# Attention in a hybrid layer: turns of the weight tiles in the row halves of the array, value products in bursts of two units

## What is computed

```python
def _stick_breaking(q, k, v):
    q = q.astype(f32) * (d ** -0.5)
    for blk in range(S // Q_BLOCK):
        z = jnp.einsum('bthd,bshd->bhts', qb, kb)
        strict = jnp.arange(t1)[None, :] < jnp.arange(t0, t1)[:, None]
        log_beta = jax.nn.log_sigmoid(z)
        log_keep = jnp.where(strict, jax.nn.log_sigmoid(-z), 0.0)
        after = lax.cumsum(log_keep, axis=3, reverse=True) - log_keep
        A = jnp.where(strict, jnp.exp(log_beta + after), 0.0)
        outs.append(jnp.einsum('bhts,bshd->bthd', A, vb))
```

## Time and profile before

| | |
|---|---|
| median of 3 runs | 3558.57 us (3555.73 to 3559.9) |
| profiled execution, span from first to last instruction | 3554.5 us |
| PE busy in it | 3472.8 us, 98% |
| DVE, ACT, POOL busy | 2494.5, 1944.9, 651.6 us |
| mean granted TensorE clock | 0.989 of full speed |

### The profile page before, as it was taken

One profiled execution on the slowest core, in us unless ns is written; L12 is line 12 of the kernel. 1 busy time (PEld: TensorE's weight loads), 2 busy tenths in 40 slices (PEclk: granted clock), 3 DMA queues, 4 the chain that ended last, 5 costly groups with the idle time before them and its releaser, 6 DMA issues. The chain is left out here.

```text
span 3554.5 us, 66436 instructions
## 1 busy us (share of the span) xinstructions
PE 3472.8 (98%) x24178; PEld 2810.3 (79%) x24178; DVE 2494.5 (70%) x3501; ACT 1944.9 (55%) x4049; POOL 651.6 (18%) x677
## 2 busy tenths in 40 slices
PE   7998999999999999989999999999999999999998
PEld 4777888999999978867777777777777777788887
DVE  4664446334688862349898989899889989666665
ACT  4553223222444432237777777777777777555554
POOL 2312332100000024300103010300021002232332
PEclk8999999999999999989999999999999999999999
DMA  8989779877756689850012101210111001666663
GB/s 285 334 313 333 257 258 313 275 238 249 269 182 190 214 292 315 301 198 19 19 49 71 33 19 39 60 43 29 38 55 49 12 29 39 190 206 192 205 211 130
DMA packets 415584, 582.24 MB, mean 164 GB/s; under 512 B 35568, under 2 KB 298096, under 8 KB 414288
## 3 DMA queue, kind: packets, MB, share of 16 engines
q1 hardware_dynamic: 394560, 506.56, 43.3%
q0 software_dynamic: 16960, 58.73, 4.8%
q10 hardware_dynamic: 3792, 13.30, 1.0%
HBM read 393.74 MB, written 184.75 MB: 163 GB/s over the span
## 5 line engine op out<-in xcount | busy, mean ns | idle before, releaser
L1467 DVE TENSOR_TENSOR_SCAN a_prod<-a_keep,a_prod,a_zeros 128x512 f32<-128x512 f32 x896 | 1077.4, 1269 | 95.3 <-ACT a_keep L1398 92.9
L1407 ACT COPY a_turned<-a_rt 128x512 f32<-128x512 f32 x1088 | 547.2, 588 | 237.7 <-PE a_rt L1327 237.3
L1398 ACT ACTIVATE a_keep<-a_z 128x512 f32<-128x512 f32 (+3 forms) x1152 | 555.4, 572 | 41.2 <-PE a_z L1316 40.9
L1327 PEld LDWEIGHTS a_rt<-c_ident,a_prod 128*128 128x128 f32 x4224 | 452.7, 141 | 114.2 <-issue 56.1
L1327 PE MATMUL a_rt<-c_ident,a_prod 128*128 128x128 f32 x4224 | 532.3, 278 | 5.0 <-DVE a_prod L1467 3.7
L1340 PE MATMUL a_acc<-a_turned,c_dw 128*64 128x256 f32 x4352 | 519.6, 380 | 2.5 <-ACT a_osum L1417 2.5
L1340 PEld LDWEIGHTS a_acc<-a_turned,c_dw 128*64 128x64 f32 x4352 | 286.6, 136 | 214.7 <-issue 91.7
L1316 PE MATMUL a_z<-c_khi,a_q 64*128 64x512 f32 (+3 forms) x2304 | 372.8, 402 | 14.0 <-DMA c_dw<-scratch_dw 12.5
L939 DVE TENSOR_TENSOR p_hlo<-p_wraw,p_hlo 128x1024 fp32r<-128x1024 f32 x85 | 105.6, 1242 | 321.5 <-ACT p_hlo L704 321.5
L704 ACT CAST p_hlo<-p_wraw 128x1024 fp32r<-128x1024 f32 x85 | 89.1, 1049 | 391.5 <-PE p_bank L572 209.0
L1292 POOL TENSOR_SCALAR_AFFINE_SELECT a_keep<-a_keep 128x256 f32<-128x256 f32 x128 | 72.7, 571 | 1235.4 <-ACT a_keep L1398 1232.0
(11 more groups left out here) (297 smaller groups left out, 6257.3 us busy)
## 6 DMA issues: line engine op xcount, KB each, us to landing
p_hlo<-scratch_parts SPq DMA_DIRECT2D x130, 512.0 KB, 5.2
p_wraw<-scratch_sums SPq DMA_DIRECT2D x128, 512.0 KB, 6.7
p_aslot<-scratch_parts SPq DMA_DIRECT2D x62, 512.0 KB, 4.8
p_u<-in_w_in POOLq DMA_DIRECT2D x64, 256.0 KB, 5.8
scratch_wsums<-p_u POOLq DMA_DIRECT2D x32, 512.0 KB, 6.9
p_hraw<-scratch_sbv POOLq DMA_DIRECT2D x32, 512.0 KB, 7.3
m_xt<-in_x SPq DMA_DIRECT2D x32, 512.0 KB, 5.3
out_y<-c_pair SPq DMA_DIRECT2D x32, 512.0 KB, 4.6
```

The lines of the kernel that those rows point to most:

```text
L1327: last = pe.transpose(rt[k % RB][:, h * QW + i * P:h * QW + (i + 1) * P], prod[:, u % PB, 2 * i + h, kb * P:(kb + 1) * P], ident[:])
L1398: act.activation(keep[:, at % KB, 0:w], z[at % ZB][:, 0:w], ACT.Sigmoid, scale=-Z_SCALE).then_inc(keep_done, 1)
L1407: act.copy(by_head(turned[:, k % TB]), by_head(rt[k % RB][:])).then_inc(turned_done, 1)
L1467: dve.tensor_tensor_scan(prod[:, u % PB, s, 0:w][:, ::-1], keep[:, at % KB, 0:w][:, ::-1], zeros[:, 0:w], first, ALU.mult, ALU.add).then_i ...
```

## The change

PE's `turn` now takes two key blocks (a pair) at a time. Each 128x128 block is turned in two halves of 64 queries: the rows 0 to 63 of the `a_prod` tile lie in the upper row half of the array, the rows 64 to 127 in the lower one, each half with 128 columns of weights and 64 columns of identity. All upper halves of a pair (8 slots of 64) fill one bank of `a_rt` and all lower halves the next one, and the pair signals `rt_done` once. ACT's `copies` takes the pair with two copies, one per bank, which write runs of 64 elements so that the halves lie side by side again; where the second block of a pair counts for one query tile only, each of them becomes two smaller copies. `a_turned` is a ring of six pairs (12 key blocks).

The order within a step changes: PE does turn(u, 0), scores(u+2), turn(u, 1), and then the value products, but these only in the steps that `WEIGH_AT` names: the units of a row are taken two by two, and both are weighed in the step after the second (a row with an odd number of units has a single one at its end). ACT does copies(u, 0), gates(u+2), copies(u, 1); row_out follows in the step after the value products. The waits: pair k waits for `turned_done` >= 2k - 1, two counts per pair.

The small tiles of the opening are no longer tiles of their own but lie in the last two slots of `a_turned`; before ACT writes there for the first time (k == 4) it waits for the store of `m` (`m_out`) and for the last of the gate steps (`g_const` 7).

```diff
--- before.py
+++ after.py
@@ -1123,7 +1123,7 @@
                 UNITS.append((hp, row, cb, j))
     NU = len(UNITS)
     ZB, RB = 4, 3
-    KB, PB, TB = 8, 3, 8
+    KB, PB, TB = 8, 3, 6
     SPLIT_AT = ((), (0,), (1,), (2,), (3,), (4, 5), (6, 7), ())
     GATE_AT = ((), (0,), (1,), (2,), (3,), (), (), ())
 
@@ -1139,11 +1139,18 @@
     def skip(u, kb):
         return max(0, kb - UNITS[u][2] % 2 * 2) if diag(u) else 0
 
+    HB = P // 2
     FIRST, OWNER = [], []
     for u in range(NU):
         FIRST.append(len(OWNER))
-        OWNER += [u] * blocks(u)
+        OWNER += [u] * (blocks(u) // 2)
     FIRST.append(len(OWNER))
+    WEIGH_AT = [[] for _ in range(NU + 1)]
+    for row in range(len(LAST)):
+        first = LAST[row - 1] + 1 if row else 0
+        for u in range(first, LAST[row] + 1, 2):
+            last = min(u + 1, LAST[row])
+            WEIGH_AT[last + 1] += range(u, last + 1)
 
     with ExitStack() as ctx:
         sb = lambda n, s, dt=F32: ctx.enter_context(nc.sbuf_tensor("a_" + n, s, dt))
@@ -1153,15 +1160,16 @@
         khi, klo, dw, pair, ident, ones, maskb, xw, xs, bm = (held[k] for k in ("khi", "klo", "dw", "pair", "ident", "ones", "maskb", "xw", "xs", "bm"))
         keep = sb("keep", [P, KB, CH])
         prod = sb("prod", [P, PB, 4, CH])
-        turned = sb("turned", [P, TB, CH])
+        turned = sb("turned", [P, TB, 2, CH])
         zeros = sb("zeros", [P, CH])
         osum = sb("osum", [P, 2, QW])
-        vrow, v_e = sb("vrow", [NT, SH * SD]), sb("v_e", [P, NP * NT])
-
-        ig, fg, soft, b, u_g, top, m = (sb(n, [P, P]) for n in ("ig", "fg", "soft", "b", "u", "top", "m"))
+        v_e = sb("v_e", [P, NP * NT])
         mcol_in = sb("mcol_in", [P, 1])
-        b_before, tops, mlast_row, mprev_row = (sb(n, [1, MH, NT]) for n in ("b_before", "tops", "mlast_row", "mprev_row"))
-        mlast = sb("mlast", [P, MH, NT])
+        opening = turned[:, 4:6].rearrange("p a b t -> p (a b t)")
+        vrow = opening[0:NT, 0:SH * SD]
+        ig, fg, soft, b, u_g, top, m = (opening[:, CH + k * P:CH + (k + 1) * P] for k in range(7))
+        b_before, tops, mlast_row, mprev_row = (opening[0:1, CH + k * P:CH + (k + 1) * P].rearrange("a (h c) -> a h c", h=MH) for k in range(7, 11))
+        mlast = opening[:, CH + 11 * P:CH + 12 * P].rearrange("p (h c) -> p h c", h=MH)
         wout_raw, wgate = pair[:, 0], pair[:, 1]
         wpart = sb("wpart", [P, QW])
         z = [ps(f"z{k}", [P, CH]) for k in range(ZB)]
@@ -1317,15 +1325,19 @@
                             if part == 2:
                                 mm.then_inc(z_done, 1)
 
-            def turn(u):
+            def turn(u, pair):
+                k = FIRST[u] + pair
                 pe.wait_ge(scan_done, 4 * u + 4)
-                for kb in range(blocks(u)):
-                    k = FIRST[u] + kb
-                    after(pe, turned_done, k + 1 - RB)
+                after(pe, turned_done, 2 * k + 2 - RB)
+                for b in range(2):
+                    kb = 2 * pair + b
                     for h in range(2):
                         for i in range(skip(u, kb), 2):
-                            last = pe.transpose(rt[k % RB][:, h * QW + i * P:h * QW + (i + 1) * P], prod[:, u % PB, 2 * i + h, kb * P:(kb + 1) * P], ident[:])
-                    last.then_inc(rt_done, 1)
+                            at = (4 * b + 2 * h + i) * HB
+                            for half in range(2):
+                                rows = slice(half * HB, (half + 1) * HB)
+                                last = pe.transpose(rt[(2 * k + half) % RB][:, at:at + HB], prod[rows, u % PB, 2 * i + h, kb * P:(kb + 1) * P], ident[rows, rows])
+                last.then_inc(rt_done, 1)
 
             def weigh(u):
                 _, row, cb, j = UNITS[u]
@@ -1333,11 +1345,11 @@
                     pe.wait_ge(g_act, 8)
                 if diag(u):
                     after(pe, row_done, row)
-                pe.wait_ge(turned_done, FIRST[u + 1])
+                pe.wait_ge(turned_done, 2 * FIRST[u + 1])
                 for kb in range(blocks(u)):
                     for h in range(2):
                         lo = skip(u, kb) * P
-                        last = pe.matmul(acc[h * SD:(h + 1) * SD, lo:QW], dw[:, h, j * TPC + kb, :], turned[:, (FIRST[u] + kb) % TB, h * QW + lo:(h + 1) * QW],
+                        last = pe.matmul(acc[h * SD:(h + 1) * SD, lo:QW], dw[:, h, j * TPC + kb, :], turned[:, (FIRST[u] + kb // 2) % TB, kb % 2, h * QW + lo:(h + 1) * QW],
                                          start=diag(u) and kb == 0, stop=j == 0 and kb == blocks(u) - 1, skip_group_check=True)
                 last.then_inc(av_done, 1)
 
@@ -1359,12 +1371,15 @@
             pe.matmul(acc[:, 2 * P:3 * P], ones[0:1, :], row(mlast_row), start=True, stop=True).then_inc(g_pe, 1)
             pe.wait_ge(g_act, 4)
             for u in range(NU):
-                turn(u)
+                turn(u, 0)
                 if u + 2 < NU:
                     scores(u + 2)
-                if u:
-                    weigh(u - 1)
-            weigh(NU - 1)
+                if blocks(u) > 2:
+                    turn(u, 1)
+                for w in WEIGH_AT[u]:
+                    weigh(w)
+            for w in WEIGH_AT[NU]:
+                weigh(w)
 
         @block.scalar
         def _(act):
@@ -1397,14 +1412,22 @@
                     after(act, scan_done, at + 1 - KB)
                     act.activation(keep[:, at % KB, 0:w], z[at % ZB][:, 0:w], ACT.Sigmoid, scale=-Z_SCALE).then_inc(keep_done, 1)
 
-            def copies(u):
-                for kb in range(blocks(u)):
-                    k, lo = FIRST[u] + kb, skip(u, kb) * P
-                    act.wait_ge(rt_done, k + 1)
-                    if k >= TB:
-                        act.wait_ge(av_done, OWNER[k - TB] + 1)
-                    by_head = lambda t: t.rearrange("p (h q) -> p h q", h=2)[:, :, lo:] if lo else t
-                    act.copy(by_head(turned[:, k % TB]), by_head(rt[k % RB][:])).then_inc(turned_done, 1)
+            def copies(u, pair):
+                k, short = FIRST[u] + pair, skip(u, 2 * pair + 1)
+                act.wait_ge(rt_done, k + 1)
+                if k == 4:
+                    act.wait_ge(m_out, 16)
+                    act.wait_ge(g_const, 7)
+                if k >= TB:
+                    act.wait_ge(av_done, OWNER[k - TB] + 1)
+                for half in range(2):
+                    src = rt[(2 * k + half) % RB][:].rearrange("p (s t) -> p s t", t=HB)
+                    dst = turned[:, k % TB].rearrange("p b (s e t) -> p (b s) e t", e=2, t=HB)[:, :, half]
+                    if short:
+                        act.copy(dst[:, 0:4], src[:, 0:4])
+                        act.copy(dst[:, 5:8:2], src[:, 5:8:2]).then_inc(turned_done, 1)
+                    else:
+                        act.copy(dst, src).then_inc(turned_done, 1)
 
             def row_out(u):
                 hp, row, cb, _ = UNITS[u]
@@ -1421,13 +1444,16 @@
             gates(1)
             columns()
             for u in range(NU):
-                if u >= 2:
-                    row_out(u - 2)
-                copies(u)
+                if u >= 1:
+                    for w in WEIGH_AT[u - 1]:
+                        row_out(w)
+                copies(u, 0)
                 if u + 2 < NU:
                     gates(u + 2)
-            row_out(NU - 2)
-            row_out(NU - 1)
+                if blocks(u) > 2:
+                    copies(u, 1)
+            for w in WEIGH_AT[NU - 1] + WEIGH_AT[NU]:
+                row_out(w)
 
         @block.vector
         def _(dve):
```

## The result

The changed kernel takes 3567.15 us (median of 14 runs, 3557.73 to 3571.37), the kernel before beside it 3558.44 (14 runs, 3555.06 to 3561.03). The ratio is 1.0021, 95% interval 1.0014 to 1.0028: slower by 9 us. The forecast was 3642 us, 83 slower, and its range began at 3600.

What follows compares the result with a forecast made beforehand. The prediction took PE's own program order in the attention stage as the bound. Borders -95, half turns +8, new wait +174, small waits -4 gave +83 us: 3559 + 83 = 3642 us, forecast 3600 to 3685, range ending at 3700.

Steps and rivals of the forecast that it cites:

- half turns 0.08 apart or less: Attention turns: the pace of half-turn pairs, in us, that the prediction said would show it wrong.
- its own sum: Attention stage total: -95 + 8 + 174 - 4 = +83 us, giving 3642 us.
- the wait: Attention steps without value products: PE waits 1.44 us for ACT's copy behind four gates, 128 steps, +174 us in all.
- Rival (b): Steps without value products: the wait is hidden and only the border gain stays, 3468 us; chance 3%.
- (d): ACT's copies of turned blocks: runs of 64 cost 0.24 us more each, 92 us more, 3734 us; chance 5%.
- the borders: PE's switches between turns, scores and value products cost 0.18 us each; having fewer gains 95 us.
- Rival (e): Borders between turns and scores stay, caused by something other than the cut: +58, 3700 us; chance 4%.
- I take 0.111 a pair: Attention turns: pairs of half turns come 0.111 us apart, judged by score rows, +8 us in all.
- rival (a): Attention turns: half turns stream faster, 0.055 us a pair, gaining 179 us, 3463 us; chance 6%.
- its rule that the sign turns below 0.085 a pair: Attention turns: half-turn pairs closer than 0.085 us would make the change not slower, over 3200 blocks.

Runs made afterwards that it cites:

- Experiment 4: Changed kernel plus six small unused products behind the scores of each step without value products: 3529.63 us, ratio 0.9915 to the kernel before.
- Experiment 2: Changed kernel with ACT doing two of the four gates before the second pair's copies and two after: 3465.3 us, ratio 0.9741 to the kernel before.
- experiment 1: Changed kernel with each unit's value products run in the step after it, no double bursts: 3420.55 us, ratio 0.961 to the kernel before.
- experiment 6: Kernel before, turns kept whole, with only the double bursts of value products and the ring of six pairs added: 3603.2 us, ratio 1.0129.
- experiment 9: Changed kernel with value products unit by unit and turns of only the first 32 rows of each half: 3435 us, ratio 0.9651 to the kernel before.

## Why the prediction was right in its sign and wrong in its size

**The sign was luck.** The prediction named what would show it wrong, half turns 0.08 apart or less, and they came 0.062 apart. With this pace its own sum gives 3642 - 3200 x 0.049 = 3485 us, faster than before. Two things that are not in this sum brought the time back up: the lower clock, 44 us, and a gain of the pace that was some 45 us smaller than this sum makes it. Experiment 4, with the clock up, is faster than before by 29 us. So the sign came out as forecast by a cost that was not forecast. (The range of the forecast is given once to 3685 and once to 3700; the measured time is below both.)

**Right: the wait.** PE waits in the steps without value products, behind four gates, for the first copy of the second pair. Foreseen were 4.67 us from turn to turn and 128 waits of 1.4; measured are 4.43 us in the step shown (4.39 from scores to scores), and waits of up to 1.8 us, 180 + 34 us in 107 + 23 entries. The gates took 1.91 (2007.35 to 2009.26, foreseen 1.92). Experiment 2 moved two gates and the step fell by two gates; experiments 1 and 6 show that the double bursts cause it with either kind of turn. Rival (b), no wait, is out, and so is the fear that copies in runs of 64 cost more (d): two cover 1.07 to 1.14, 0.6 for one as in the earlier trace rows. DVE, busy 1274 of 1433 us, did not bind in the changed kernel.

**Right: the borders.** Between turns and scores in the 64x128 cut the "issue" entries are gone, as said from the earlier trace rows; what stays is that the first two pairs of scores take 0.55 us (experiment 1, 2000.20 to 2000.75 for scores after turns) where two pairs take 0.46, of which I had counted 0.06. Rival (e) is out, and experiment 9 shows the cause from the other side: another height, and the border is there again.

**Wrong: the pace of the half turns.** The failed step is "I take 0.111 a pair", from the narrow scores of the earlier trace rows. It is 0.062. The bounds given (0.055 to 0.218) held it, and rival (a) had the pace nearly right (0.055) but got 6 chances in 100. Its time, 3463 us, did not come either, nor its rule that the sign turns below 0.085 a pair. The choice of the nearest row was the mistake: I took the row with the same cut and the same width of weights, and passed over the kind of load. The sign of that was in the trace of before. A load of a turn lasts 140 ns; a load of the scores, as the prediction itself notes, 0.19 us. In the mix stage of before both kinds stand in the whole array with the same 128x128 operands (groups by form: busy us, mean ns of one; L1635 are turns, L1650 plain products):

```profile
L1650 PEld LDWEIGHTS mp_n<-c_dw,m_pm 128*128 128x128 f32 x256 | 38.9, 192 | 2.2 <-DVE m_pm L1820 2.2
...
L1635 PEld LDWEIGHTS mp_t<-c_ident,m_hf 128*128 128x128 f32 x128 | 15.9, 140 | 4.2
```

Same rows, same columns, 192 ns against 140: the length of a load goes with its kind, not with the cut, and I took the pace of one kind for the other. Whole turns come every 0.109 us with 128 columns streamed, so they could not tell whether load or stream set that; the load's length could have told that scores were the wrong neighbour, and the forecast should have lain between the two ends, with a range down to rival (a).

The Trainium skill (TensorE: Matmul & The Clock Gate, LDWEIGHTS) gives a load its columns/1.2 ns, 107 ns for 128 columns, whatever the rows. For the plain loads the trace agrees (0.112 a pair). For the turns' loads it doesn't (0.062 a pair), and there the measurement decides.

**Not foreseen: the clock.** The prediction counted a wait as its own length. A PE that idles 1.8 of 4.4 us in every second step is granted the lower clock now and then, and the work after it, which has no idle time to lose, takes longer. It costs 44 us (experiment 4). From 1597 to 3030 the trace of before could not show it, since PE hardly idled there. But at the opening of the stage it did: PE waits 12.5 us there, until 1576.06, the clock is at its lower level (0.50 from 1570 to 1590), and two pairs of scores take 0.85 us (1577.16 to 1578.01) where they take 0.46 otherwise.

```profile
1576.06 1.01 PE L1316 MATMUL a_z<-c_khi,a_q 64*128 64x384 f32 x4 [12.54 <-DMA c_dw<-scratch_dw]
...
1577.16 1.08 PE L1316 MATMUL a_z<-c_khi,a_q 64*128 64x512 f32 x4
1578.01 0.66 PE L1316 MATMUL a_z<-c_klo,a_q 64*128 64x512 f32 x2
```

**The sum.** Foreseen: 128 steps without values at 578 us (100 at 4.67, 12 at 4.6, 16 at 3.5) and, with before's 1431 and the 83 more, 936 us for the others. The first are 35 us less: the first copy starts 0.76 after the first turn (2005.63, 2006.39) where I had 1.13, and of these 0.37 some 0.14 are lost again, since the next turn follows the start of the second pair's copies after 0.80 (2009.26, 2010.06) where I had 0.66. The others are 77 us less where the clock stays up (experiment 4, 859 us). The pace explains it: 272 groups of eight pairs in those 160 steps, each 0.37 shorter, make 100 us; the 23 between I can't assign. Then the clock takes 44 back: 83 - 35 - 77 + 44 = +15 us, and the two profiled executions are 14 apart. So the small result is no small effect. It is two gains (borders and pace) and two losses (wait and clock) that happen to meet.

**Where the gain of the pace would have gone.** In the steps that wait for ACT, PE's faster turns only make the wait longer: 1.77 for the 1.44 foreseen. That is why 0.37 us in each of 528 groups of eight pairs, some 195 us of PE's time, left so little.

The version to keep is experiment 1, 3420.55 us, 3.9% under the kernel before and 4.1% under the changed one; the split of the gates adds nothing that can be measured.

## What to carry to other kernels

When an edit thins out a periodic piece of work (here every second step has no value products), look at the steps that are left without it: what hid behind that piece on the other engines is now waited for, and each burst that was saved took two borders of 0.18 us with it and brought a wait of up to 1.8 us. Price an operation that the trace doesn't show by a row of the same kind of instruction first, and only then by one of the same shape. And a wait on TensorE has a second price, the lower clock of the work behind it; filling it with idle products can win that back, but taking the wait away wins more (38 us in experiment 4, 147 in experiment 1).

## What the runs showed of the hardware that was not expected

- Loads for a turn and plain loads have different costs for the same columns: two loads of 128 columns, one in each row half, follow the last two after 0.062 us as turns (0.061 with 32 rows in place of 64) and after 0.112 us as plain float32 products. One lasts 138 to 143 ns as a turn's, 184 to 198 as a plain one's.
- A plain product of float32 operands with 64 or 128 columns streamed shows up as two passes; a turn is one.
- Turns of 32 rows between products of 64 rows bring a border of some 0.1 us on each side back (0.32 for 0.23 ahead of the turns, 0.61 for 0.52 from the turns to the scores); with turns of 64 rows it is not there.
- With waits of 1.8 us in every second step the granted clock fell to its lower level in 30 short stretches, 102 us from 1597 to 3030; with six small products in each of these waits it fell once; with the gates split it fell four times, each time after 1.8 to 2.0 us of idle time. With turns of 64 rows and waits up to 1.3 us (experiment 1) it did not fall in the stage, with turns of 32 rows (experiment 9) it fell seven times after 0.7 to 1.2 us. So the length of the wait is not all that counts; what else does is open.
